# Closing the scopes of a two-layer backbone without their second barrier, and making its constants inside the first block

## What is computed

```python
for layer in range(DEPTH):                      # DEPTH = 2
    hl, hc = modulate(rmsnorm(xl, g), ...), modulate(rmsnorm(xc, g), ...)
    if layer % 2 == 0:                          # retention heads + RG-LRU
        oc, ol = ab_mixer(hc, hl, ...)
    else:                                       # latent attention, 16 heads
        oc, ol = mla_mixer(hc, hl, ...)
    xl = xl + mod_l[2] * ol                     # (context too in layer 0)
    y = hier_moe(tokens, group_w, expert_w, w_gate, w_up, w_down)
    xl = xl + mod_l[5] * y
return rmsnorm(xl, final_norm_g)
```

## Time and profile before

| | us |
|---|---|
| median of 3 runs | 1989.86 (1988.77 to 1990.26) |
| the profiled execution, its own time | 1985.21 |
| its span, first to last instruction | 1982.8 |
| PE busy / DVE / ACT / POOL | 1710.8 / 788.9 / 411.0 / 263.4 |
| mean granted TensorE clock | 0.93 of full |

### The profile page before, as it was taken

The page is one execution under the profiler, slowest core; times in us unless marked ns, Lnnn a source line. Parts: engine busy times, 40 slices in busy tenths (PEclk is TensorE's granted clock), DMA queues, the critical chain, the costliest instruction groups (busy, mean ns, idle before and its releaser), DMA issues. The chain is left out here.

```text
span 1982.8 us, 26424 instructions
## 1 busy us (share of the span) xinstructions
PE 1710.8 (86%) x9052; PEld 879.3 (44%) x9053; DVE 788.9 (40%) x1326; ACT 411.0 (21%) x778; POOL 263.4 (13%) x380
## 2 busy tenths in 40 slices
PE   5999999898999799996669999999978799755555
PEld 2454445655445344443346455555533344333332
DVE  3787795755212111111135347775432111211213
ACT  3204644110001101111123145553100000000002
POOL 1113541200101000000023410000011000000101
PEclk8999999999899899998779999999989899877777
DMA  9976665334699999999972010003569999999994
GB/s 371 345 286 238 224 230 206 118 136 188 266 383 404 418 420 418 414 417 410 425 299 92 0 76 31 1 1 101 224 252 406 412 415 413 415 415 417 420 414 173
DMA packets 104198, 559.92 MB, mean 282 GB/s; under 512 B 21780, under 2 KB 41968, under 8 KB 64568
## 3 DMA queue, kind: packets, MB, share of 16 engines
q1 hardware_dynamic: 90304, 519.55, 65.7%
q0 software_dynamic: 7744, 20.98, 3.0%
q10 hardware_dynamic: 6072, 18.36, 2.4%
HBM read 523.19 MB, written 40.91 MB: 284 GB/s over the span
## 5 line engine op out<-in xcount | busy, mean ns | idle before, releaser
L2339 PE MATMUL exp_gps<-home_pieces,all_hT 128*32 128x256 f32 x672 | 105.9, 485 | 88.5 <-DMA home_pieces<-in_moe_w_up 82.1
L690 PE MATMUL abp_ps<-home_pieces,all_hT 128*128 128x512 f32 x384 | 168.8, 596 | 0.0
L2510 DVE TENSOR_TENSOR all_hT<-all_hT,exp_ups 64x512 f32<-64x512 f32 (+1 forms) x30 | 20.7, 690 | 343.4 <-PE exp_ups L2352 180.9
L2508 DVE TENSOR_TENSOR all_hT<-all_hT,exp_ups 64x256 f32<-64x256 f32 x34 | 14.4, 425 | 271.1 <-ACT all_hT L2441 262.0
L2356 PE MATMUL exp_gps<-home_pieces,all_hT 128*64 128x512 f32 x176 | 88.8, 663 | 31.8 <-DMA home_pieces<-in_moe_w_up 29.2
L690 PEld LDWEIGHTS abp_ps<-home_pieces,all_hT 128*128 128x128 f32 x384 | 71.7, 190 | 96.9 <-issue 95.4
L2339 PEld LDWEIGHTS exp_gps<-home_pieces,all_hT 128*32 128x32 f32 x672 | 46.5, 138 | 136.9 <-issue 122.7
L2343 PE MATMUL exp_ups<-home_pieces,all_hT 128*32 128x256 f32 x672 | 106.0, 485 | 1.3 <-issue 1.3
L2299 POOL COPY exp_idx<-all_tok 128x1 int32 (+1 forms) x58 | 10.4, 180 | 696.7 <-DVEq L2499 696.7
L1600 PE MATMUL att_sc<-mlakv_KT,home_pieces 96*128 96x384 f32 x256 | 99.0, 510 | 2.5 <-PEq L76 1.7
L2339 PE MATMUL exp_gps<-moew_wg,all_hT 128*32 128x256 f32 x416 | 62.3, 459 | 40.3 <-DMA moew_wu<-in_moe_w_up 36.9
(11 more groups left out here) (474 smaller groups left out, 3195.8 us busy)
## 6 DMA issues: line engine op xcount, KB each, us to landing
home_pieces<-in_moe_w_gate SPq DMA_DIRECT2D x42, 2048.0 KB, 29.4
home_pieces<-in_moe_w_up SPq DMA_DIRECT2D x42, 2048.0 KB, 34.4
home_pieces<-in_moe_w_down SPq DMA_DIRECT2D x42, 2048.0 KB, 33.9
moew_wg<-in_moe_w_gate SPq DMA_DIRECT2D x22, 2048.0 KB, 28.4
moew_wu<-in_moe_w_up SPq DMA_DIRECT2D x22, 2048.0 KB, 34.8
moew_wd<-in_moe_w_down SPq DMA_DIRECT2D x22, 2048.0 KB, 32.7
all_X<-in_ada_w SPq DMA_DIRECT2D x30, 1024.0 KB, 7.1
home_pieces<-in_ada_w SPq DMA_DIRECT2D x17, 1024.0 KB, 13.9
```

The lines of the kernel that those rows point to most:

```text
L690: last = nc.tensor.matmul(ps[i % RB][:], hT[:, kk, what * P:(what + 1) * P], w[n % S][:, kk, :], start=(kk == 0), stop=(kk == KD - 1))
L2339: last_g = nc.tensor.matmul(gps[j * Q:(j + 1) * Q, 0:HC], x[:, k, 0:Q], w.g[q][:, k, j * HC:(j + 1) * HC], start=(k == 0), stop=(k == KD - 1))
```

## The change

A scope that closes hands its semaphores to a list (`Retired`) in place of clearing them; no clear and no second barrier follow. The list is cleared at three places: by POOL at the start of the `abo` block, by POOL at the start of the `mlain` block, and behind the last block, where a last barrier stays. Until then the numbers are not used again, so that later scopes get other numbers. The `const` block is gone: its four POOL instructions stand at the start of `abp`'s POOL list, and PE waits for them ahead of its first transpose.

```diff
+class Retired:
+    def __init__(self, nc):
+        self.nc, self.sems = nc, []
+    def clear(self):
+        self.nc.clear_and_free_semaphores(self.sems)
+        self.sems = []
...
     def __exit__(self, *a):
         self.stack.__exit__(*a)
-        if self.sems and a[0] is None:
-            self.nc.clear_and_free_semaphores(self.sems)
+        Scope.retired.sems += self.sems
+        if self.tag == "all" and a[0] is None:
+            Scope.retired.clear()
             self.nc.all_engine_barrier()
...
-def constants(nc, c):
-    with Scope(nc, "const") as s:
-        zeroed, made = s.sem("zeroed"), s.sem("made")
-        block = s.block()
-        @block.gpsimd
-        def _(pool):
...
-            pool.wait_ge(made, 2)
+def constants(nc, c, pool, zeroed, made):
+    nc.gpsimd.memset(c.ident[:], 0.0).then_inc(zeroed, 1)
+    nc.gpsimd.memset(c.ones[:], 1.0).then_inc(zeroed, 1)
+    pool.wait_ge(zeroed, 2)
+    nc.gpsimd.affine_select(out=c.ident[:], ...).then_inc(made, 1)
+    nc.gpsimd.affine_select(out=c.before[:], ...).then_inc(made, 1)
...
# ab_project
         @block.gpsimd
         def _(pool):
+            constants(nc, c, pool, const_zeroed, const_made)
             link = Chain(pool, pchain)
...
             after = {0: (0, 1), 1: (2,), 2: (3,), 3: (4,), 4: (5,)}
+            pe.wait_ge(const_made, 2)
             pe.wait_ge(p_ready, 16 * 5)
...
# ab_output (new POOL list) and mla_inputs (ahead of pool.wait_ge(tr_ev, NT))
+            Scope.retired.clear()
```

More of the change, by code:

```diff
@@ L66, in __init__ @@
         self.nc, self.tag, self.stack, self.sems = nc, tag, ExitStack(), []
+        if tag == "all":
+            Scope.retired = Retired(nc)
     def __enter__(self):
@@ L100, in refined_rsqrt @@
     link(V.tensor_tensor(rstd, rstd, tmp, ALU.mult))
-def constants(nc, c):
-    with Scope(nc, "const") as s:
-        zeroed, made = s.sem("zeroed"), s.sem("made")
-        block = s.block()
-        @block.gpsimd
-        def _(pool):
[L111 to L118, removed]
-            pool.wait_ge(made, 2)
+def constants(nc, c, pool, zeroed, made):
+    nc.gpsimd.memset(c.ident[:], 0.0).then_inc(zeroed, 1)
+    nc.gpsimd.memset(c.ones[:], 1.0).then_inc(zeroed, 1)
+    pool.wait_ge(zeroed, 2)
+    nc.gpsimd.affine_select(out=c.ident[:], in_=c.ident[:], compare_op=ALU.not_equal, fill=1.0,
+                            base=0, pattern=[[-1, P]], channel_multiplier=1).then_inc(made, 1)
+    nc.gpsimd.affine_select(out=c.before[:], in_=c.ones[:], compare_op=ALU.is_gt, fill=0.0,
+                            base=0, pattern=[[1, P]], channel_multiplier=-1).then_inc(made, 1)
 def carve(space):
@@ L473, in ab_project @@
              "ring_used", "mod_done", "stored"))
+        const_zeroed, const_made = s.sem("const_zeroed"), s.sem("const_made")
         block = s.block()
@@ L1189, in ab_output, with _ @@
         ret = rows[:, 0]
+        @block.gpsimd
+        def _(pool):
+            Scope.retired.clear()
         @block.sync
@@ L2948, in backbone @@
         c.x_ready = s.sem("x_ready")
-        constants(nc, c)
         r = routed(s)
```

## The result

The changed kernel took 1975.89 us (median of 4 runs, 1971.10 to 1982.64), the kernel before 1990.06 us beside it (4 runs, 1988.77 to 1990.27). The ratio is 0.9934 with an interval of 0.9918 to 0.9950: 10 to 16 us less. The profiled execution of the changed kernel was the slowest of its four, 1982.64 us with a span of 1979.8. Its span is only 3.0 us shorter than the one of before, 1982.8, whose execution had been 4.65 us quicker than its median. So the two spans alone say little; the profile has to be read piece by piece.

The account below looks back on a forecast made before the run. Dense blocks were taken as bound by engines handing work to each other, experts mostly by weights, with standstills at joins. 2.0 + 7.8 - 0.3 = 9.5 us off 1989.86 gave 1980.4 us, range 1975 to 1986.

Parts of the forecast that it names:

- Start: At the kernel's beginning, SP's first load leaves at about 0.85 instead of 2.85 us: 2.0 us won.
- Nine joins: Between a block's barrier release and the next block's first work, all but 0.1 us goes at nine joins: 7.8 us won.
- Moved clears: Clears in `abo` and `mlain` lie inside POOL's waits and add 0; without cover they would add 1.5 us.
- End: Behind the last block, one barrier less but larger clears and one more drain: 0.3 us lost.
- Weights' streams: At the two joins ahead of the experts, loads run dry before the saturated part, so the time won counts in full.
- Clock: PE at half clock from 331 to 334 us, behind `abp`'s join: taken as 0, with 1.5 us to both sides.
- signs of being wrong: Microsecond "issue" gaps behind joins, PE's expert weight waits growing by what was won, or clock falls in formerly full dense stretches.
- The sum: Over the whole kernel, start plus nine joins less the end: 9.5 us won.
- B: Joins ahead of the experts give nothing and the start only 0.9 us: 6.6 us won, 1983.3 us; chance 0.18.
- C: Code-fetch stalls replace barriers at joins: 1988.2 to 2002.9 us; slower 0.04, near no change 0.10 together with D.
- D: Waits left by removed barriers move into the next barrier: 1988.2 us; near no change 0.10 together with C.

Follow-up runs that it names:

- const_only: The kernel before with only the constants moved into the first block, all barriers and clears kept: 1987.38 us, ratio 0.9990.
- more_at_experts: The changed kernel with 12 further barriers at the close of `abo` and 12 at that of `mlao`, ahead of the experts: 1986.42 us, ratio 0.9983.
- again: The changed kernel once more, unaltered, beside the kernel before: 1977.85 us, ratio 0.9947.
- clears_added: The kernel before with the constants moved, all barriers and clears kept, plus clears of 90 spare semaphores in `abo` and 120 in `mlain`: 1985.25 us, ratio 0.9974.
- joins_only: The changed kernel with the block of the constants put back, so only second barriers and clears are gone: 1979.64 us, ratio 0.9950.
- again_2: The changed kernel a third time, unaltered: 1978.26 us, ratio 0.9943.
- short_end: The changed kernel with a third clear of retired semaphores, in `comb1` behind POOL's gathers: 1979.84 us, ratio 0.9946.

## Why the prediction was right

The forecast named the right causes, and their sizes come out of the profile nearly as summed. The time itself was met with less to spare: 1975.89 us is 4.5 us below the 1980.4 forecast and 0.9 above the lower end of the range, and the part beyond the sum is not explained.

**Start**, forecast 2.0: measured 1.99 at SP's first load. That the loads decide, and not POOL, is borne out by PE's first transpose, which came 1.4 us earlier, half a microsecond more than POOL won, and by `abp`'s end, 1.9 us earlier in const_only. The interval of const_only's time, 0.2 to 3.6 us, holds 2.0 and 0.9 alike.

**Nine joins**, forecast 7.8: measured 8.80 - 0.75 = 8.05. The 0.1 us left for jump and first issue was 0.08 on average, and the three joins taken by likeness were 0.73 (`mlain`), 0.71 (`att`) and 1.07 (`mlao`), less 0.1, against 0.6, 0.6 and 0.9.

**Moved clears**, forecast 0: right. The blocks that hold them were longer in some executions, but those lengths come and go without them.

**End**, forecast 0.3 lost: 0.6 lost. The three clears took 0.13, 0.22 and 0.42 us as worked out, 0.77 in all; mis-sized were the drains, three of 0.09 to 0.18 us where one more of 0.07 had been counted, and the barrier saved, 0.26 instead of 0.3.

**Weights' streams**, counted in full: borne out by more_at_experts, 6.8 to 8.6 us for 8.6 of barriers, and by the lengths of `exp0` and `exp1`, which didn't grow by what was won ahead of them. The gap in SP's issues moved with PE's first release. The two long runs of a busy DMA in the earlier trace rows are slices 11 to 19 and 30 to 38, and not 12 to 19 and 31 to 38 as the forecast has it; nothing hangs on that.

**Clock**, forecast 0 with 1.5 to both sides: the mechanism reached further than the forecast had it. It looked at one place, behind `abp`'s join. After the change this stretch has the full clock, but the fall came later in the same block:
```profile
331.00:334.00 3.00, 2.63 (x21) 1.94 (x20) 0.00 (x0) 2.23 (x6) 0.00 (x0) 1.00 1.02 410
...
349.00:352.00 3.00, 2.54 (x12) 2.57 (x13) 2.11 (x4) 0.00 (x0) 0.00 (x0) 0.60 0.02 5
352.00:355.00 3.00, 3.00 (x25) 3.00 (x24) 1.97 (x5) 0.07 (x1) 0.00 (x0) 0.83 0.00 0
```
and `ret` took 47.0 us, not less than 46.7; in again it had none of it and took 45.5. So the shorter standstill, which by the forecast could only help, did not always help; the 1.5 us that the forecast puts on this fall is the right size. The Trainium skill, page "TensorE: Matmul & The Clock Gate", Part 1, says that the throttle's phase differs from run to run, and the two executions of one program in `mlain` agree. What the forecast leaves out of account is that there are at least four such places here (`ret`, `abo`, `mlain`, `mlao`), so the scatter between two profiles can be several times the 1.5 us of one place. One of the forecast's signs of being wrong did appear, a fall of the clock where it had been full: in the profile after, `abo` and `mlain` each lost 1.6 or 1.7 us so. The forecast had no term for it, and the medians came out below it all the same, by a gain that it had no term for either.

**The sum** by measured terms is 1.99 + 8.05 - 0.6 = 9.4 us, against 9.5 forecast. The runs show more: 14.2, 12.3 and 11.3 us by the medians of three comparisons, with intervals of 10 to 16, 8 to 13 and 8.4 to 14.3. The last two hold 9.4, the first just does not. The medians lie 2 to 5 us beyond the sum, and no profile shows where. The means of the 16 executions of the changed kernel and the 35 of before beside them are 11.6 us apart, with 1.7 to both sides; that leaves 9.4 out, so the scatter of single executions alone hardly explains it. The profiled executions don't show it: in after the blocks together were 6.4 us longer than in the quick execution of before, in again 1.9. Nor does the mean granted clock of the timed executions, 0.930 in both kernels; it is a coarse measure, since most of what it lacks is lost in the expert blocks. And clears_added, which keeps all joins, also lies 3.3 us beyond the 2.0 of its start, so the removed joins need not be the reason. What a typical execution of before has more than its quick profiled one, some 5 us, no trace of it shows, and the cause stays open.

**The rivals.** B is out for the experts (more_at_experts, and joins_only's interval) and, by the profiles, for the start (PE's first transpose). C is out: behind nine jumps without a barrier the next work came within 0.02 to 0.16 us in six profiles of kernels without them, and PE's own first work within 0.07 to 0.17 us at eight of the nine in after, again and again_2. So no wait for code took the barrier's place. "Issue" waits of PE in the experts are no more than in the earlier trace rows: the largest group after is
```profile
PE exp_gps L2354 <- issue: 2.8, 2, 2.4
```
and no such wait begins at a join. The one that the row of 481.56 shows for PE's weight load, 2.46 us, ends 0.06 us behind the release, so nearly all of it lies ahead of the join. D is out: it would have left the time near 1988.2, and joins_only alone wins 7 to 13 us.

## What to carry to other kernels

A join of two blocks costs what the profile shows between the release of the block's barrier and the first work behind it, and it can be read off before anything is changed: here 0.6 to 1.5 us each, about half of it the barrier and half the clear ahead of it. Count it in full when the next block starts with all engines waiting for one another, even ahead of a long stream of weights, if the DMA share shows that the stream runs dry before its steady part, as it did here. When clears are put off, give them a place in a list that is idle anyway until the last block, since those left for the end stand on the path with a drain each.

Before two profiles are compared by their spans, lay out the lengths of their blocks and look at the granted clock where one has grown: the same program differed here by 2.7 us in one block. And see where the profiled execution lies among the timed ones, since a profile of a quick execution can hide several microseconds.

## What was not expected of the hardware

A standstill of 4 us cost more than its own time where dense matmuls followed: 24 barriers of 0.34 to 0.38 us took 6.8 to 8.6 us of time ahead of the experts and 12.2 to 14.0 us (1991.80 less 1979.60, 1978.26 or 1977.85) ahead of dense blocks. The halved clock at the start of `abo` and `mlao` goes with 3.2 us of the difference in the profiles.

A drain of POOL in front of a clear took 0.05 to 0.20 us elsewhere, but 7.07 us behind the gathers in `comb1` (short_end), on an engine that nobody waited for. Where another engine waits for POOL, such a clear would have to be expected to cost that time; no run here tests it.
```profile
L69 POOLq DRAIN  x3: 85/97/7067, 1950.1 to 1957.8; - x3
```
